# The launch of a transformer-like block: other load order, x transposed by tiles, three input blocks side by side, one and a half modulation chunks summed on VectorE

## The reference

```python
mod = (silu(c) @ w_ada + b_ada)                      # 6 * 1024 columns, 12 chunks of 512
sh_m, sc_m, g_m, sh_f, sc_f, g_f = split(mod, 6)
u = layer_norm(x) * (1 + sc_m) + sh_m                # 1024 x 1024
z = u @ w_in                                         # pooling, q, k, v, convolution, gates
...                                                  # three branches, merged, w_o, residual, LN
u = layer_norm(x) * (1 + sc_f) + sh_f                # then the squared-ReLU MLP and a last LN
```

## Time and profile before

| what | us |
|---|---|
| median of 3 runs | 1433.06 (1431.15 to 1433.45) |
| the profiled execution | 1431.08 |
| its span, first to last instruction | 1429.3 |
| PE busy | 1401.4 (98%) |
| DVE busy | 965.6 (68%) |
| ACT busy | 634.6 (44%) |
| POOL busy | 420.1 (29%) |
| PE's share of the chain that ended last | 83% |

### The profile page before, as it was taken

The page is one execution under the profiler, slowest core; times in us unless marked ns, Lnnn a source line. Parts: engine busy times, 40 slices in busy tenths (PEclk is TensorE's granted clock), DMA queues, the critical chain, the costliest instruction groups (busy, mean ns, idle before and its releaser), DMA issues.

```text
span 1429.3 us, 17335 instructions
## 1 busy us (share of the span) xinstructions
PE 1401.4 (98%) x6554; PEld 1150.8 (81%) x6554; DVE 965.6 (68%) x1334; ACT 634.6 (44%) x902; POOL 420.1 (29%) x453
## 2 busy tenths in 40 slices
PE   6999999999999999999999999999999999999996
PEld 1788788888878888888888888888888888888885
DVE  3877677776579955365668797565665746447687
ACT  3412577787541224111616774433445535343251
POOL 1005356556556000000024317434444200001215
PEclk9999999999999999999999999999999999999998
DMA  9883454665565322762632455444445978466361
GB/s 347 276 292 120 133 171 154 184 182 159 162 218 171 112 90 77 245 191 90 199 126 89 160 181 195 143 146 155 162 155 207 302 257 301 169 222 235 111 228 59
DMA packets 159035, 256.42 MB, mean 179 GB/s; under 512 B 11304, under 2 KB 81374, under 8 KB 158952
## 3 DMA queue, kind: packets, MB, share of 16 engines
q1 hardware_dynamic: 144104, 204.97, 42.9%
q0 software_dynamic: 14848, 50.34, 10.5%
HBM read 182.36 MB, written 68.71 MB: 176 GB/s over the span
## 4 chain that ended last, share of the span: by engine, by line
PE 83%; DVE 9%; DMA 2%; ACT 2%; issue 2%; SPq 1%; POOL 0%; DVEq 0%; ACTq 0%; POOLq 0%
PE ps L1977 22%; PE ps L1979 22%; PE ps L1978 22%; PE ps L2105 10%; PE ps L2145 2%; PE ps L2155 2%; PE ps L2170 2%; DVE bn L1330 1%; DMA mid<-in_x_dram 1%; DVE mid L1710 1%; DMA t_raw<-u_scratch 1%; DVE part_lo L1834 1%; DVE partial L1381 1%; DVE mix_tmp L1703 1%; PE ps L2044 1%
## 5 line engine op out<-in xcount | busy, mean ns | idle before, releaser
L1977 PE MATMUL ps<-act_hi,w_hi 128*128 128x512 f32 (+1 forms) x496 | 192.6, 388 | 0.4 <-DVE w_lo L1841 0.4
L1979 PE MATMUL ps<-act_hi,w_lo 128*128 128x512 f32 (+1 forms) x496 | 190.2, 384 | 0.0
L1978 PE MATMUL ps<-act_lo,w_hi 128*128 128x512 f32 (+1 forms) x496 | 190.0, 383 | 0.0
L1834 DVE TENSOR_TENSOR part_lo<-k_raw,part_hi 128x1024 fp32r<-128x1024 f32 x112 | 146.5, 1338 | 56.1 <-ACT part_hi L897 53.4
L1978 PE MATMUL ps<-part_lo,part_hi 128*128 128x512 f32 x448 | 174.3, 389 | 0.0
L1977 PE MATMUL ps<-part_hi 128*128 128x512 f32 x448 | 174.3, 389 | 0.0
L1979 PE MATMUL ps<-part_hi,part_lo 128*128 128x512 f32 x448 | 174.3, 389 | 0.0
L897 ACT ACTIVATE part_hi<-k_raw 128x1024 fp32r<-128x1024 f32 x112 | 116.4, 1059 | 110.6 <-DMA k_raw<-tw_scratch 48.9
L1324 DVE TENSOR_TENSOR w_lo<-w_raw,w_hi 128x1024 fp32r<-128x1024 f32 x52 | 68.5, 1316 | 68.4 <-ACT w_hi L897 68.3
L1977 PEld LDWEIGHTS ps<-act_hi,w_hi 128*128 128x128 f32 x496 | 93.4, 188 | 19.2 <-issue 0.7
L1978 PEld LDWEIGHTS ps<-act_lo,w_hi 128*128 128x128 f32 x496 | 93.5, 188 | 18.5 <-issue 1.0
(11 more groups left out here) (249 smaller groups left out, 3168.7 us busy)
## 6 DMA issues: line engine op xcount, KB each, us to landing
k_raw<-h_scratch SPq DMA_DIRECT2D x112, 256.0 KB, 4.5
ada<-in_w_ada_dram SPq DMA_DIRECT2D x11, 2048.0 KB, 9.4
w_raw<-in_w_in_dram SPq DMA_DIRECT2D x42, 512.0 KB, 4.5
tw_rows<-in_w_ff_dram POOLq DMA_DIRECT2D x64, 256.0 KB, 4.1
tw_scratch<-tw_sum POOLq DMA_DIRECT2D x32, 512.0 KB, 3.4
h_scratch<-h_sum POOLq DMA_DIRECT2D x64, 256.0 KB, 2.8
k_raw<-tw_scratch SPq DMA_DIRECT2D x64, 256.0 KB, 5.5
pair_raw<-in_w_ff_dram SPq DMA_DIRECT2D x13, 1024.0 KB, 6.1
```

The source lines that it names most:

```text
L1834: nc.vector.tensor_tensor(part_lo[s][:, :, :], k_raw[rs][:, :, :], f(part_hi[s][:, :, :]), ALU.subtract)\
L1977: nc.tensor.matmul(out, sh, mh, start=first, stop=False)
L1978: nc.tensor.matmul(out, sh, ml, start=False, stop=False)
L1979: return nc.tensor.matmul(out, sl, mh, start=False, stop=last)
```

## The change

- *Loads.* Chunks 0 to 3 come in halves of 1 MB. The order is: half of chunk 0, x tiles 0 and 1, the other half, tiles 2 and 3, the small rows, half of chunk 2, tiles 4 and 5, the other half, tiles 6 and 7, block 0, chunk 1, block 1, chunk 3, block 2. Before: chunk 0, tiles 0 and 1, the small rows, chunk 2, tiles 2 to 4, chunk 1, tiles 5 to 7, block 0, chunk 3, block 1.
- *x by tiles.* `transpose_x(i)` now takes all eight stretches of one tile as soon as it is normalised, and stands between the row products. ACT copies the result to a new buffer `x_t` in SBUF (the last tile is copied by DVE); the modulation reads `x_t`. The statistics go by pairs of tiles.
- *High parts of u.* Those of k = 1 to 7 are made by ACT behind each modulation; DVE makes that of k = 0 and all low parts.
- *Chunk 1.* It is summed on DVE like half of chunk 3, and PE only takes its columns.
- *Three blocks.* Block 2 has its own buffers (`third_hi`, `third_lo`, in `mid` tiles 6 and 7). Blocks 0, 1 and 2 are computed side by side in banks 4, 2 and 0: first their parts of k = 0 to 3, then the columns of chunks 1 and 3, then the parts of k = 4 to 7. Blocks 3 to 5 follow; chunks 4 and 5 are reduced after block 3, chunks 6 and 7 after block 5.

PE before the first product: the rows on the engine before, from the chunk 2 on (L1996 row products, L2007 columns, L2044 transposes).

The diff, cut to its core. Loads on SP:

```diff
+                if i == 3:
+                    sp.wait_ge(head_ps_done, 1)
+                elif i == 4:
+                    sp.wait_ge(partial_done, 1)
+                elif i == 5:
+                    sp.wait_ge(head_ps_done, 4)
+                elif i == 6:
+                    sp.wait_ge(head_ps_done, 5)
+                    sp.wait_ge(partial_done, 2)
                 elif i >= 7:
                     sp.wait_ge(partial_done, i - 2 - N_DIRECT)
...
+            load_ada_half(0, 0)
             load_x(range(2))
+            load_ada_half(0, 1)
+            load_x(range(2, 4))
...
-            load_ada(2)
-            load_x(range(2, 5))
+            load_ada_half(2, 0)
+            load_x(range(4, 6))
+            load_ada_half(2, 1)
+            load_x(range(6, ST))
+            load_block(0)
             load_ada(1)
-            load_x(range(5, ST))
-            load_block(0)
...
             load_ada(4)
-            sp.wait_ge(rel_done, 1)
-            sp.dma_start(rel_dram, rel_ext[:, :]).then_inc(scratch_stored, 16)
-            for n in range(2, 9):
-                load_ada(n + 3)
+            load_block(3)
+            load_ada(5)
+            for n in range(4, 9):
+                load_ada(n + 2)
                 load_block(n)
```

The buffers, and ACT:

```diff
+    x_t = at("x_t", [P, KT, SEQ], f32, 32 * KB)
...
+    third_hi = at("third_hi", [P, KT, P], f32r, 88 * KB)
+    third_lo = at("third_lo", [P, KT, P], f32r, 92 * KB)
...
+            def modulate_x(k):
                 if k >= 2:
                     act.wait_ge(u_lo_done, k - 1)
-                act.wait_ge(z_done, k + 1)
-                nc.scalar.activation(u_tmp[k % 2][:, :], banks(2 * (k % 2)), ACT.Identity, bias=mod[:, k:k + 1],
-                                     scale=mod[:, KT + k:KT + k + 1]).then_inc(u_tmp_done, 1)
-
-            for n in range(N_P1):
-                act.wait_ge(z_done, KT + n + 1)
-                src = banks(4 if n == 0 else 2 * (n % 2))
+                nc.scalar.activation(u_tmp[k % 2][:, :], x_t[:, k, :], ACT.Identity, bias=mod[:, k:k + 1],
+                                     scale=mod[:, KT + k:KT + k + 1]).then_inc(u_step, 1)
+                if k >= 1:
+                    act.wait_ge(u_step, 2 * k)
+                    copy(act_hi[:, k, :], u_tmp[k % 2][:, :]).then_inc(u_step, 1)
+
+            act.wait_ge(mod_done, 1)
+            act.wait_ge(x_copied, ST)
+            for k in range(3):
+                modulate_x(k)
+            cut_hi(1)
+            modulate_x(3)
+            cut_hi(2)
+            save_ada_row(3)
+            act.wait_ge(mod_done, 2)
+            for k in range(4, KT):
+                modulate_x(k)
+
```

DVE:

```diff
+            mixer_columns(0)
+            dve.wait_ge(z_done, ST)
+            nc.vector.tensor_copy(x_t[:, :, (ST - 1) * P:ST * P], tile_banks(ST - 1)).then_inc(x_copied, 1)
+            cut_lo(0)
+            cut_u_lo(0)
+            cut_u_lo(1)
+            cut_lo(1)
+            cut_u_lo(2)
+            start_chunk(1)
+            cut_u_lo(3)
+            end_chunk(1)
+            cut_lo(2)
+            ada_chunk(3)
+            mixer_columns(1)
+            cut_u_lo(4)
+            start_chunk(4)
+            for k in range(5, KT):
+                cut_u_lo(k)
+            end_chunk(4)
+            cut_lo(3)
+            dve.wait_ge(small_in, SMALL_BIASES)
+            nc.vector.tensor_copy(rel_ext[:, 2 * REL_CLIP:768],
+                                  rel_ext[:, 2 * REL_CLIP - 1:2 * REL_CLIP]
+                                  .to_broadcast([HEADS, 768 - 2 * REL_CLIP])).then_inc(rel_done, 1)
...
+            start_chunk(5)
+            take_glu(0)
+            end_chunk(5)
+            cut_lo(4)
+            ada_chunk(6)
+            take_glu(1)
+            cut_lo(5)
+            gate_chunk(4)
+            gate_chunk(5)
+            ada_chunk(7)
+            ada_chunk(8)
+            cut_lo(6)
+            ada_chunk(9)
+            cut_lo(7)
+            pool_means(0)
 
             def cut_lo_after(pair, r):
```

PE:

```diff
+            def transpose_x(i):
+                if i < ST - 1:
+                    pe.wait_ge(normed, i + 1)
+                else:
+                    pe.wait_ge(norm_end, 1)
+                if i >= 2:
+                    pe.wait_ge(x_copied, i - 1)
+                for k in range(KT):
+                    ins = nc.tensor.transpose(tile_banks(i)[:, k, :], mid[:, i, k * P:(k + 1) * P], ident[:, :])
+                ins.then_inc(z_done, 1)
+
...
-            row_chunk(2)
+            row_chunk(0, 0)
+            transpose_x(0)
+            transpose_x(1)
+            row_chunk(0, 1).then_inc(head_ps_done, 1)
+            transpose_x(2)
+            transpose_x(3)
+            pe.wait_ge(small_in, SMALL_ROWS)
+            nc.tensor.transpose(ps[:, 7, PIECE:PIECE + ROWS_A], rows_a[:, :], ident[0:ROWS_A, 0:ROWS_A])\
+                .then_inc(head_ps_done, 1)
+            nc.tensor.transpose(ps[:, 7, PIECE + P:PIECE + P + ROWS_C], rows_c[:, :], ident[0:ROWS_C, 0:ROWS_C])\
+                .then_inc(head_ps_done, 1)
+            row_chunk(2, 0)
+            transpose_x(4)
             row_columns(0)
+            transpose_x(5)
+            row_chunk(2, 1).then_inc(head_ps_done, 1)
+            transpose_x(6)
             row_columns(2)
-            row_chunk(1)
-
...
+            def rows_part(n, k):
                 pe.wait_ge(u_lo_done, k + 1)
                 for h in range(2):
-                    ins = product(ps[:, 4 + h, :], (w_part(0, k), act_part(k, half_cols(h))), k == 0, k == KT - 1)
-                if k == 1:
-                    row_columns(3)
-            ins.then_inc(z_done, 1)
-            for n in range(1, N_P1):
-                if n >= 2:
-                    pe.wait_ge(w_lo_done, n + 1)
-                if n == 2:
-                    pe.wait_ge(u_tmp_done, KT)
-                elif n == 1:
-                    pe.wait_ge(u_lo_done, KT)
+                    ins = product(ps[:, P1_BANKS[n] + h, :], (w_part(n, k), act_part(k, half_cols(h))),
+                                  k == 0, k == KT - 1)
+                if k == KT - 1:
+                    ins.then_inc(z_done, 1)
+
+            pe.wait_ge(w_lo_done, 1)
+            for k in range(2):
+                rows_part(0, k)
+            pe.wait_ge(w_lo_done, 2)
+            for k in range(2):
+                rows_part(1, k)
+            for n in range(2):
+                for k in range(2, 4):
+                    rows_part(n, k)
+            pe.wait_ge(mod_done, 1)
+            row_chunk(3, 0).then_inc(head_ps_done, 1)
+            pe.wait_ge(w_lo_done, 3)
+            for k in range(4):
+                rows_part(2, k)
+            row_columns(1)
+            row_columns(3)
+            for k in range(4, 6):
+                for n in (1, 0, 2):
+                    rows_part(n, k)
+            for n in (1, 0, 2):
+                for k in range(6, KT):
+                    rows_part(n, k)
+
+            for n in range(3, N_P1):
+                pe.wait_ge(w_lo_done, n + 1)
+                if n == 3:
+                    pe.wait_ge(mod_done, 2)
...
-                    reduce_chunk(n + 2)
-                    reduce_chunk(n + 3)
+                if n == 3:
+                    reduce_chunk(4)
+                    reduce_chunk(5)
+            pe.wait_ge(glu_done, 2)
+            reduce_chunk(6)
+            reduce_chunk(7)
 
             def project(pair, m):
```

More of the change, by code:

```diff
@@ L338, in block_used @@
             if n < N_P1:
-                return z_done, 8 + n + 1
+                return z_done, ST + P1_END[n]
             if n < N_G:
@@ L920, in save_ada_row, with save_tile @@
             def save_ada_row(i):
-                act.wait_ge(head_ps_done, (1, 5, 4, 6)[i])
+                act.wait_ge(head_ps_done, {0: 1, 2: 4, 3: 5}[i])
                 copy(ada_row[i], ps[0:1, ADA_BANKS[i], :]).then_inc(head_sb_done, 1)
-            for i in range(ST + 1):
-                if i < ST:
-                    take_root(i, i)
-                if 1 <= i < ST:
-                    norm(i - 1, i - 1, mid[:, i - 1, :])
+            def save_tile(i):
+                act.wait_ge(z_done, i + 1)
+                copy(x_t[:, :, i * P:(i + 1) * P], tile_banks(i)).then_inc(x_copied, 1)
@@ L2048, in _ @@
[L2048 to L2064 removed]
+            transpose_x(7)
```

268 lines of the change are left out of this document (132 added, 136 removed).

## The result

| | before | changed |
|---|---|---|
| median, same chip, 20 runs each (us) | 1431.43 | 1433.87 |
| profiled execution (us) | 1431.08 | 1435.17 |
| its span (us) | 1429.3 | 1433.4 |
| start of the first projection (us) | 122.53 | 125.21 |

The changed kernel takes 1.0016 times as long, with a 95% interval of 1.0010 to 1.0022: 2.4 us more. Of the 2.6 us between forecast and result, 1.6 is the median of three runs (1433.06) from which I started: against the before of the same 20 runs (1431.43) my term of +3.5 us would have given 1434.9. The profiled execution of the changed kernel is the slowest of its twenty.

The account below looks back on a forecast made before the run. PE bounds the kernel, busy 98% of the span. First product 3.7 us sooner, then added waits, make the first projection +1.8 us later; one clock hole of 1.7 makes +3.5, from median 1433.06 to 1436.5 us, range 1429 to 1442.

Parts of the forecast that it names:

- my term of +3.5 us: Launch up to the first projection: +1.8 us from work and waits plus 1.7 for one clock hole.
- the likeliest case: Whole kernel slower by +2.9 to +6 us, 1435.9 to 1439; chance 0.42.
- no measurable change: Rival: same mechanism, but no clock hole or a 1 to 2 us wait missing; 0 to +1.8 us, chance 0.27.
- First product: PE's first input-block product starts at 41.0 us, 3.7 us sooner than before.
- The waits of 2.0 and 1.0: Among the first parts, PE waits 2.0 us for block 1's lower weights and 1.0 for k 3's lower part.
- The gap for k 4: Behind the columns of chunks 1 and 3, PE idles 4.3 us for k 4's modulation, cast and lower part.
- The clock: Launch's granted clock: one hole, 1.7 us, bounded by 0 and 3.4; a skill rule says long PE waits bring it.
- slower by more: Rival: low clock also in PE's preparation and a second hole after the gap; +6.9 us, 1440, chance 0.14.
- The three blocks' end: Blocks 0, 1 and 2 end at 88.2 us against 86.32 before.
- DVE's cover: Blocks 3 to 5: DVE's lower weights come before PE asks, price nothing; at most some 2 us if cover went.
- The loads: Launch loads: last x tile lands at 27.7 instead of 33, but earlier x buys little; late-load rival given no chance.
- The signs: Launch timeline: first product near 41, 4 us gap at 67 to 72, block 1 wait at 44, launch end 124 to 126.

Follow-up runs that it names:

- experiment 3: Changed kernel plus five fp32 matmuls, results unused, in PE's wait before the first product; 1433.92 us, ratio 1.0017 to the kernel before.
- experiment 1: Changed kernel with the columns of chunks 1 and 3 computed after block 2's first part instead of its fourth; 1429.22 us, 0.9985 of the kernel before.
- 4: Changed kernel with PE's half row product of chunk 3 before the first product and columns after block 2's second part; 1428.25 us, 0.9981 of the kernel before.
- 5: Changed kernel with chunk 3's half row product before the first product, its load early, columns after block 2's second part; 1425.83 us, 0.9960 of the kernel before.
- 8: Changed kernel with chunk 3's half row product before the first product and its load early, columns left late; 1429.91 us, 0.9988 of the kernel before.
- experiment 2: Changed kernel plus 16 matmuls, results unused, behind the columns of chunk 3, filling PE's gap; 1432.81 us, 1.0009 of the kernel before.
- experiment 7: Changed kernel with only slices 0 and 7 of chunk 1 summed on DVE, six left out; 1432.16 us, 1.0004 of the kernel before.
- experiment 6: Changed kernel with the load order of the kernel before, halves of a chunk back to back; 1441.21 us, 1.0064 of the kernel before.

## Why the prediction was right, step by step

The sign and the main mechanism held: a launch that starts its products sooner and gives it back in one gap behind the late columns. The number is in part luck, because errors in the sum offset each other. And what was measured, +2.4 us and 1433.87, lies under the likeliest case (+2.9 to +6, 0.42) and in the range of the rival *no measurable change* (0.27). That rival had two conditions, no hole or a missing wait of 1 to 2 us: the second came true, for both short waits, and the first did not, since there were two holes.

- *First product.* Forecast 41.0, measured 39.05. Mis-sized by 2 us at the loads: the half chunk landed at 6.72 (forecast 8.4) and tile 0 at 8.17 (9.8). I had carried the rate of 0.385 MB per us back from the landing at 11.1; in the changed kernel tile 1, with the same 2.1 MB asked for by then, is taken at 9.81 without a wait. Why the pieces land sooner is open. From the end of the transposes on, the steps take 4.8 us, as forecast. (My 16.6 for tile 1 is 16.8 by its own terms.)
- *The waits of 2.0 and 1.0.* Hidden in the changed kernel, present at 1.52 and 0.77 in experiment 3. What failed is that I priced the products ahead of them at full clock: at half speed these cover the waits.
- *The gap for k 4.* Forecast 4.3, measured 4.15. Experiments 1, 4 and 5, which take it away, make the kernel faster than before, and 8, which leaves it, has it at 4.15 again.
- *The clock.* Forecast one hole of 1.7, behind the gap. Measured two of 12 products at 0.43 instead of 0.23, so 2.5 us each. The first costs nothing (experiment 3). The second is paid, since nothing waits behind it; how much of it filling the gap gives back is known only roughly (experiment 2, 1.7 us in one profile). Its place was wrong too: it begins in the columns, ahead of the gap. The rule of the Trainium skill, "TensorE: Matmul & The Clock Gate", section "HAM oscillation — how this bites in real kernels", agrees with the first hole: it came behind a 4.7 us wait in the changed kernel, and the filler of experiment 3 removed it. For the second it is not enough: experiment 1 has the fall and no wait.
- *A low clock in the preparation* (the rival *slower by more*). The first eight row matmuls take 5.50 us against 3.59 for the next eight, as the first five were slow before. That costs nothing: PE still waits 0.89 us for tile 0 behind them. From there to the last transposes at 34.3 the windows show 1.00 and eight transposes take about 1.0 us each time. (The windows show 1.00 over the slow row matmuls as well, so the granted clock on record does not explain them.)
- *The account.* From the forecast with one hole, 126.0, to 125.21: first product −1.95, waits 4.15 for 7.3, so −3.15, clock 5.1 for 1.7, so +3.4; that leaves +0.9 that I cannot assign. The medians differ by 2.44, near the 2.68 of the projection's start, so in the median the launch's loss is carried to the end nearly unchanged. In the two profiled executions it is not: their spans differ by 4.1.
- *The three blocks' end.* Forecast 88.2, measured 89.0.
- *DVE's cover.* Lower weights of blocks 4, 5 and 6 were forecast at about 94, 102 and 116 and start at 93.42, 101.59 and 117.25; PE does not wait for them. Experiment 7 bounds the price at 1.7 us.
- *The loads.* I gave them no price of their own, and wrote that the earlier x buys little. Without the new order the changed kernel would lose 7.3 us more (experiment 6). The forecast did not need it, since I worked with the new order throughout, but as a term it was missed.
- *The signs.* Of those that I had set, the gap, the third block's end (88 to 90) and the launch's end (124 to 126) came as stated; the first product was 0.45 us earlier than its stretch (39.5 to 42.5), and the wait for block 1's weights at 44 did not show.

## What to carry to other kernels

When a chain of small steps (reduce, scale, cast, subtract) leads from one instruction of the bounding engine to another of its own, put enough independent work of that engine between the two: the columns moved three parts earlier were worth 4.7 us here in the median, 3.5 in the launch. Where an engine waits at the start, look for work that stands later on its path and whose data can be loaded in time (row chunk 3: 4.0 us). And before a wait or a low clock is repaired, ask what comes second: experiment 3 removed a low clock and gained nothing.
